# A two-layer decoder trunk on one Trainium2 core: a partial product copied from PSUM bank to PSUM bank in the FFN's Strassen-like blocks, the product order changed, and two waits of the first blocks

## The reference: what is computed

```python
D_MODEL = 1024; SEQ = 512; DEPTH = 2; D_FF = 2816
...
for l in range(DEPTH):
    ...
    x = x + mix @ w_out[l]
    h2 = rms_norm(x, ffn_norm[l])
    gate, up = jnp.split(h2 @ w_gate_up[l], 2, axis=-1)
    x = x + (jax.nn.silu(gate) * up) @ w_down[l]
```

## Time and profile before

| what | value |
|---|---|
| median of 3 runs | 1340.62 us (1340.58 to 1340.69) |
| the profiled execution's own time | 1340.9 us |
| its span in the trace | 1339.2 us |
| PE busy | 1327.0 us, 99% of the span |
| VectorE, ScalarE, GpSimd busy | 791.4, 626.2, 659.8 us |
| chain that ended last | PE 89%, DVE 5%, POOL 2%, ACT 2% |

### The profile page before, as it was taken

The page is one execution under the profiler, slowest core; times in us unless marked ns, Lnnn a source line. Parts: engine busy times, 40 slices in busy tenths (PEclk is TensorE's granted clock), DMA queues, the critical chain, the costliest instruction groups (busy, mean ns, idle before and its releaser), DMA issues.

```text
span 1339.2 us, 22389 instructions
## 1 busy us (share of the span) xinstructions
PE 1327.0 (99%) x8936; PEld 1166.1 (87%) x8936; DVE 791.4 (59%) x1480; ACT 626.2 (47%) x1207; POOL 659.8 (49%) x454
## 2 busy tenths in 40 slices
PE   8999999999999999999999999999999999999999
PEld 7888887778799889998879888887888998899987
DVE  5637777723987138881165387777249861488711
ACT  5563436634556225652335543466335652256511
POOL 4458307644455544554343663176434554454552
PEclk9999999999999999999999999999999999999999
DMA  7315400114243324333222352001232323334322
GB/s 171 124 40 158 102 10 1 33 53 84 76 112 109 104 87 113 109 95 118 87 85 77 75 167 66 1 5 30 63 95 83 107 96 110 95 95 118 104 87 86
DMA packets 176584, 114.92 MB, mean 86 GB/s; under 512 B 48224, under 2 KB 154976, under 8 KB 176480
## 3 DMA queue, kind: packets, MB, share of 16 engines
q1 hardware_dynamic: 174368, 113.22, 29.8%
q10 hardware_dynamic: 2112, 0.26, 0.1%
HBM read 109.80 MB, written 3.67 MB: 85 GB/s over the span
## 4 chain that ended last, share of the span: by engine, by line
PE 89%; DVE 5%; POOL 2%; ACT 2%; issue 1%; DMA 1%; SPq 0%; DVEq 0%; ACTq 0%
PE ps L795 31%; PE ps L1280 29%; PE ps L1181 7%; PE ps L845 6%; PE ps L1082 2%; PE ps L934 2%; PE ps L1125 2%; PE ps L1108 2%; DVE arena L2441 1%; ACT sT_hi L1403 1%; PE ps L860 1%; PE ps L1134 1%; POOL arena L1900 1%; PE ps L914 1%; PE ps L1043 1%
## 5 line engine op out<-in xcount | busy, mean ns | idle before, releaser
L1805 POOL TENSOR_TENSOR w_lo<-w_raw,w_hi 128x2048 fp32r<-128x2048 f32 (+2 forms) x59 | 264.3, 4479 | 313.3 <-ACT w_hi L1382 246.0
L1382 ACT ACTIVATE w_hi<-w_raw 128x2048 fp32r<-128x2048 f32 (+2 forms) x61 | 113.8, 1866 | 236.7 <-PE ps L795 160.8
L1821 POOL TENSOR_TENSOR aT_lo<-ffn_tmp,aT_hi 128x512 fp32r<-128x512 f32 x44 | 58.2, 1322 | 180.7 <-ACT aT_hi L1425 180.7
L2556 DVE SCALAR_TENSOR_TENSOR x_tok<-ps,st,x_tok 128x512 f32<-128x512 f32 x32 | 23.8, 749 | 144.3 <-PE ps L795 144.3
L2459 DVE TENSOR_TENSOR ps<-w_raw 128x512 f32<-128x512 f32 x76 | 88.0, 1158 | 24.3 <-DMA w_raw<-in_w_gate_up 24.3
L795 PE MATMUL ps<-w_hi,aT_hi 128*128 128x512 f32 x352 | 95.8, 390 | 0.0
L795 PE MATMUL ps<-w_lo,aT_hi 128*128 128x512 f32 x352 | 95.4, 389 | 0.0
L795 PE MATMUL ps<-w_hi,aT_lo 128*128 128x512 f32 x352 | 95.4, 389 | 0.0
L795 PE MATMUL ps<-hT_hi,w_lo 128*128 128x512 f32 x320 | 81.0, 393 | 0.0
L1390 ACT ACTIVATE w_hi<-w_raw 128x512 fp32r<-128x512 f32 x38 | 24.0, 632 | 118.4 <-PE ps L1280 89.9
L795 PEld LDWEIGHTS ps<-w_lo,aT_hi 128*128 128x128 f32 x352 | 66.1, 188 | 13.9
(11 more groups left out here) (385 smaller groups left out, 3344.5 us busy)
## 6 DMA issues: line engine op xcount, KB each, us to landing
w_raw<-in_w_gate_up SPq DMA_DIRECT2D x88, 512.0 KB, 5.1
w_raw<-in_w_in SPq DMA_DIRECT2D x21, 1024.0 KB, 5.4
w_raw<-in_w_down SPq DMA_DIRECT2D x16, 1024.0 KB, 5.1
w_raw<-in_w_down SPq DMA_DIRECT2D x8, 768.0 KB, 4.5
w_raw<-in_w_out SPq DMA_DIRECT2D x16, 256.0 KB, 4.0
w_raw<-in_w_out SPq DMA_DIRECT2D x8, 512.0 KB, 5.0
w_raw<-in_w_in SPq DMA_DIRECT2D x2, 1056.0 KB, 7.4
x_tok<-in_x SPq DMA_DIRECT2D x4, 512.0 KB, 5.4
```

Of the source, the lines that this page charges most:

```text
L1382: nc.scalar.activation(whi[:, c % 2, 0:kt * w], raw[:, c % 2, 0:kt * w], ACT.Copy).then_inc(S["w_hi"], 1)
L1805: nc.gpsimd.tensor_tensor(wlo[:, c % 2, 0:kt * w], raw[:, c % 2, 0:kt * w], whi[:, c % 2, 0:kt * w].bitcast(F32), ALU.subtract).then_inc(S ...
L1821: nc.gpsimd.tensor_tensor(alo[:, cnt % FT, :], ft[:, cnt % 2, :], ahi[:, cnt % FT, :].bitcast(F32), ALU.subtract).then_inc(S["a_lo"], 1)
```

## The change

In a fast block, ScalarE copies product one from bank X directly into bank Y (PSUM to PSUM) instead of to SBUF, and TensorE accumulates S2*T2 on top of it. u2_add on VectorE is gone, and with it the SBUF tile p1c. S1*T1 (bank Z) becomes the second product and S2*T2 (bank Y) the third. copy_p5 comes ahead of copy_u2 in ScalarE's list; z_add and t_lo(c + 1, 1) change places in VectorE's. Beside this, plain block 2 no longer waits for gsc and up_mul (i >= 2 becomes i >= 3), since banks 0 and 1 have no earlier block in them; and for block 3 GpSimd does the first quarter's low part ahead of block 1's activation low part.

```diff
 block_product(c, "A11", "B11", X, True, False).then_inc(S["prod"], 1)
 if cnt == N_PLAIN:
-    pe.wait_ge(*S.at("up_mul", N_PLAIN - 1, l))
     pe.wait_ge(*S.at("sum_lo", 4, l))
-elif cnt == FT:
+if cnt == FT:
     pe.wait_ge(*S.at("x_down", 8, l))
-pe.wait_ge(*S.at("sum_lo", 4 + 4 * j + 2, l))
-block_product(c, "S2", "T2", Y, True, False).then_inc(S["prod"], 1)
-if cnt != FT:
+else:
     pe.wait_ge(*S.at("up_mul", halves_done(cnt - 1, 0), l))
+pe.wait_ge(*S.at("sum_lo", 4 + 4 * j + 1, l))
 block_product(c, "S1", "T1", Z, True, False).then_inc(S["prod"], 1)
 pe.wait_ge(*S.at("p_copy", 3 * j + 1, l))
+pe.wait_ge(*S.at("sum_lo", 4 + 4 * j + 2, l))
+block_product(c, "S2", "T2", Y, False, False).then_inc(S["prod"], 1)
 pe.wait_ge(*S.at("w_lo", splits(c), l))
 block_product(c, "A12", "B21", X, False, True).then_inc(S["prod"], 1)
-pe.wait_ge(*S.at("p_copy", 3 * j + 2, l))
+pe.wait_ge(*S.at("p_copy", 3 * j + 3, l))
...
-                        if i >= 2:
+                        if i >= 3:
                             pe.wait_ge(*S.at("up_mul" if s else "gsc", cnt - 1, l))
...
 def copy_p1(cnt):
     act.wait_ge(*S.at("prod", 5 * (cnt - N_PLAIN) + 1, l))
-    nc.scalar.activation(p1c, fast_bank(cnt, "X"), ACT.Copy).then_inc(S["p_copy"], 1)
+    if cnt == N_PLAIN:
+        act.wait_ge(*S.at("up_mul", N_PLAIN - 1, l))
+    elif cnt == FT:
+        act.wait_ge(*S.at("x_down", 8, l))
+    nc.scalar.activation(fast_bank(cnt, "Y"), fast_bank(cnt, "X"), ACT.Copy).then_inc(S["p_copy"], 1)
 def copy_u2(cnt):
-    act.wait_ge(*S.at("p_add", 3 * (cnt - N_PLAIN) + 1, l))
+    act.wait_ge(*S.at("prod", 5 * (cnt - N_PLAIN) + 3, l))
...
 def copy_p5(cnt):
-    act.wait_ge(*S.at("prod", 5 * (cnt - N_PLAIN) + 3, l))
+    act.wait_ge(*S.at("prod", 5 * (cnt - N_PLAIN) + 2, l))
...
+                        copy_p5(cnt)
                         copy_u2(cnt)
...
-                    if fast:
-                        copy_p5(cnt)
...
-                early = cnt is not None and 2 <= cnt < N_PLAIN
-                if early:
+                early = cnt is not None and 2 <= cnt <= N_PLAIN
+                fast = cnt is not None and is_fast(cnt)
+                if early and fast:
+                    block_lo(c, 0)
+                elif early:
                     split_lo(c)
                 if behind is not None:
                     block_a_lo(behind)
-                if cnt is not None and is_fast(cnt):
-                    block_lo(c)
+                if fast:
+                    for part in range(1 if early else 0, 2):
+                        block_lo(c, part)
...
-def u2_add(cnt):
-    dve.wait_ge(*S.at("prod", 5 * (cnt - N_PLAIN) + 2, l))
-    dve.wait_ge(*S.at("p_copy", 3 * (cnt - N_PLAIN) + 1, l))
-    Y = fast_bank(cnt, "Y")
-    V.tensor_tensor(Y, Y, p1c, ALU.add).then_inc(S["p_add"], 1)
...
-                    if fast:
-                        u2_add(cnt)
                     if prepare:
                         t_sum(c + 1, 3)
                         t_lo(c + 1, 0)
+                        t_lo(c + 1, 1)
                     if fast:
                         z_add(cnt)
-                    if prepare:
-                        t_lo(c + 1, 1)
```

More of the change, by code:

```diff
@@ L72 @@
     "x_res": 8, "zgate": 1, "zth": 1,
-    "prod": 95, "p_copy": 57, "p_add": 57, "sum": 77, "sum_hi": 80, "sum_lo": 80,
+    "prod": 95, "p_copy": 57, "p_add": 38, "sum": 77, "sum_hi": 80, "sum_lo": 80,
 }
@@ L262, in trunk @@
         p5c = pbuf[:, 2048:2304]
-        p1c, u2c = (raw[:, s, KD * 256:KD * 256 + 256] for s in range(2))
+        u2c = raw[:, 1, KD * 256:KD * 256 + 256]
         gtm = at(0, NT, 3 * GW)
@@ L1296, in fast_block @@
                 if cnt == N_PLAIN:
-                    pe.wait_ge(*S.at("up_mul", N_PLAIN - 1, l))
                     pe.wait_ge(*S.at("sum_lo", 4, l))
-                elif cnt == FT:
+                if cnt == FT:
                     pe.wait_ge(*S.at("x_down", 8, l))
-                pe.wait_ge(*S.at("sum_lo", 4 + 4 * j + 2, l))
-                block_product(c, "S2", "T2", Y, True, False).then_inc(S["prod"], 1)
-                if cnt != FT:
+                else:
                     pe.wait_ge(*S.at("up_mul", halves_done(cnt - 1, 0), l))
+                pe.wait_ge(*S.at("sum_lo", 4 + 4 * j + 1, l))
                 block_product(c, "S1", "T1", Z, True, False).then_inc(S["prod"], 1)
                 pe.wait_ge(*S.at("p_copy", 3 * j + 1, l))
+                pe.wait_ge(*S.at("sum_lo", 4 + 4 * j + 2, l))
+                block_product(c, "S2", "T2", Y, False, False).then_inc(S["prod"], 1)
                 pe.wait_ge(*S.at("w_lo", splits(c), l))
                 block_product(c, "A12", "B21", X, False, True).then_inc(S["prod"], 1)
-                pe.wait_ge(*S.at("p_copy", 3 * j + 2, l))
+                pe.wait_ge(*S.at("p_copy", 3 * j + 3, l))
                 pe.wait_ge(*S.at("sum_lo", 4 + 4 * j + 4, l))
                 block_product(c, "S3", "T3", Y, False, False).then_inc(S["prod"], 1)
-                pe.wait_ge(*S.at("p_add", 3 * j + 2, l))
+                pe.wait_ge(*S.at("p_add", 2 * j + 1, l))
                 block_product(c, "S4", "B22", Z, False, True).then_inc(S["mm"], 1)
-                pe.wait_ge(*S.at("p_add", 3 * j + 3, l))
+                pe.wait_ge(*S.at("p_add", 2 * j + 2, l))
                 block_product(c, "A22", "T4", Y, False, True).then_inc(S["mm"], 1)
@@ L1806, in split_lo, with block_lo @@
                                         whi[:, c % 2, 0:kt * w].bitcast(F32), ALU.subtract).then_inc(S["w_lo"], 1)
-            def block_lo(c):
+            def block_lo(c, part):
                 dst, src, hi = (slot(v, c, KD, 256) for v in (wlo, raw, whi))
-                pool.wait_ge(*S.at("w_hi", splits(c) - 1, l))
-                nc.gpsimd.tensor_tensor(dst[:, 0:4, 0:P], src[:, 0:4, 0:P], hi[:, 0:4, 0:P].bitcast(F32), ALU.subtract
-                                        ).then_inc(S["w_lo"], 1)
+                if part == 0:
+                    pool.wait_ge(*S.at("w_hi", splits(c) - 1, l))
+                    nc.gpsimd.tensor_tensor(dst[:, 0:4, 0:P], src[:, 0:4, 0:P], hi[:, 0:4, 0:P].bitcast(F32), ALU.subtract
+                                            ).then_inc(S["w_lo"], 1)
+                    return
                 pool.wait_ge(*S.at("w_hi", splits(c), l))
@@ L2499, in gate_up @@
                 if is_fast(cnt):
-                    dve.wait_ge(*(S.at("p_add", 3 * (cnt - N_PLAIN) + 3, l) if h else S.at("mm", mm_count(chunk_of(cnt)) - 1, l)))
+                    dve.wait_ge(*(S.at("p_add", 2 * (cnt - N_PLAIN) + 2, l) if h else S.at("mm", mm_count(chunk_of(cnt)) - 1, l)))
                     g, up = token_half(g, h), p5c if h else fast_bank(cnt, "Z")
```

## The result

The changed kernel takes 1349.12 us in the median (1348.61 to 1351.23, 4 runs), the kernel before, run beside it, 1340.61 us (1340.58 to 1340.69): ratio 1.0066, 95% interval 1.0054 to 1.0079. It is slower by 8.5 us; the forecast was 2.4. The profiled execution took 1349.19 us.

What follows compares the result with a forecast made beforehand. TensorE was taken as the bound, busy 1327.0 of 1339.2 us. Steady blocks 0 and +1.22 a layer, +2.4 in all, gave a 1341.6 span, 1343.3 profiled, 1343.1 for the runs; range 1341.9 to 1346.1.

Steps and rivals of the forecast that it cites:

- Steady blocks cost 0: Fast blocks: new product order and PSUM copy add no TensorE wait, cost 0, the copy's slack being 0.86 us.
- Block 3 starts 2.06 earlier: Without plain block 2's two waits, block 3 starts at 360.23 instead of 362.29, 2.06 us won for the moment.
- The gap moves to S1*T1: Block 3's second product waits for bank Z, released by VectorE's gate_up of block 2; a gap of about 3.5 us.
- the +1.44 a layer: If VectorE's list kept its times, six products instead of five follow the wait in block 3: block 4 starts 1.44 later.
- T3's t_sum of block 3 is stalled by GpSimd: VectorE at 359.05 finds GpSimd in B11's low part, ends at 360.17 instead of 359.74, and is 0.43 late.
- The tie at T1 of block 4 goes to VectorE: VectorE at 363.07 beats GpSimd at 363.08; S1*T1 starts at 365.13, block 4 at 373.85: +1.22 us a layer.
- the other side of the tie: GpSimd gets in first at T1 of block 4: S1*T1 at 366.30, +2.4 a layer; one or both layers, chance 0.27.
- The clock stays full in the new gap: TensorE's clock was taken to stay full behind block 3's gap, adding nothing to the forecast sum.
- rival 4: TensorE's clock falls in block 3's new gap: two slower products a layer, +8.2, 1348.8; one a layer 1346.0; chance 0.05.
- Rivals priced one by one: GpSimd winning the tie (1344.3 or 1345.4, chance 0.27) and the clock falling (1348.8 or 1346.0, 0.05) were priced separately.
- The sum has no term outside the FFN: The forecast added only +1.22 us a layer at block 3 of the FFN, with no term for the mixer.

Runs made afterwards that it cites:

- the filler: Changed kernel plus 16 unused 256-column matmuls in block 3's gap, between the copy of product one and the wait for gate_up: 1347.38 us, ratio 1.0051.

## Why the prediction was wrong, step by step

- **Steady blocks cost 0: right.** 924 matmuls take 110.73 us, the copy from bank to bank 0.37 us, its slack 0.87. Copy and product order are worth nothing to them, for or against: 110.73 us with them and 110.71 without, and with block 3 in TensorE's order 1337.3 and 1337.49 us for the whole kernel.
- **Block 3 starts 2.06 earlier, at 360.23: right.** It starts at 360.17.
- **The gap moves to S1*T1, behind gate_up of block 2: right.** Another bank for it takes 8.6 us off the total. With block 2's waits and GpSimd's old order back, the product order and its copy cost the +1.44 a layer that was worked out.
- **T3's t_sum of block 3 is stalled by GpSimd: right**, 1.12 us, with 1.1 predicted.
- **The tie at T1 of block 4 goes to VectorE: wrong.** This is the step that the forecast rested on. VectorE was 0.02 us behind GpSimd and not 0.01 ahead, and the stall is 1.12 us. S1*T1 starts at 366.25, where the other side of the tie gave 366.30. The size was right and the side was not; hundredths cannot be had from sums of rows that are rounded to hundredths, and the chance of 0.27 for it was too small against 0.50. Two of the kernels above, with the same list up to this point, have VectorE 0.01 to 0.02 us ahead instead. That is +1.1 a layer.
- **The clock stays full in the new gap: wrong.** This is rival 4, to which I gave 0.05. The reason given, that no row of before shows a fall, was no evidence: before had no gap above 0.90 us there. Worth +1.49 and +1.31; the price of one product at the lower level, 1.44 a layer, was the right size. By the Trainium skill (TensorE: Matmul & The Clock Gate, section "What's actually happening") an idle TensorE falls back to the lower clock; the trace agrees, 0.50 behind the gap of 4.49 us.
- **Rivals priced one by one: wrong.** The lost tie and the clock come together, since the tie makes the gap longer. 2 x (1.22 + 1.12) + 1.49 + 1.31 = 7.5: 1348.4 us with the 1.7 around the span and the 1339.2 under it, 0.8 below the profiled 1349.19. No rival had this case, and the range ended at 1346.1. Rival 4 names 1348.8, near the measured 1349.12, but by luck: it has the tie won and two products a layer at the lower level, 2.88 us, where the fall cost 1.3 to 1.5 and the lost tie made up the difference.
- **The sum has no term outside the FFN: wrong by 0.7.** TensorE waits 0.65 us at line 934 in layer 1, in the mixer. It is 0.3 in the kernel with gate_up first, 1.52 in the one with the filler, and absent in all others, also in the one with GpSimd's old order alone, which comes to this place as late as the changed kernel. So the lag is not the cause. The trace names no releaser, but the kernel makes this product wait for eight DMAs out of diag_out, and their times fit. The last is issued near 801.7, the longest takes 4.0 us to land, and the product starts at 805.75. Before, it is issued near 798.4, the longest takes 2.7, and the product starts at 801.18 without a wait. With gate_up first the longest takes 3.5; with the filler it is 3.1, and the DMA that fills diag_out takes 4.4 instead of 2.6. Why one execution has a slower DMA here stays open.

What is shown by undoing one thing: the bank wait, the clock's 1.45 (filler), the place of gate_up behind the contested t_sum (1.65). That the stall's 1.12 is a contest of the two engines is inferred from the pairs of times, and no run undoes it alone: in five kernels, in both layers, whoever has the earlier stamp, by 0.01 to 0.03 us, runs at its own length, and the other pays. The Trainium skill (SBUF — State Buffer, section "Who interferes with whom") says that a VectorE instruction with two SBUF inputs contends with a GpSimd instruction that reads SBUF, and that issue order decides who blocks; all ten pairs agree.

## What to carry to other kernels

Where TensorE is full, a change of order pays only at the edges of the dense stretch. Before such a change, list for every product which instruction of which other engine releases its operand and its bank, and put those instructions in each list in the order in which TensorE asks for them; a single edit moves the wait to the next product that was not moved with it, as it did here three times. A gap on TensorE of 1.9 us or more should be priced with a fall of the clock on top (1.88 us is the shortest behind which a trace here shows one). Gaps are not cheaper for being split: 1.44 and 0.25 us were harmless where 1.85 often was not, but 1.88 and 1.22 us with one product between them cost more than a single gap of 4.49. Where two engines meet within some hundredths of a microsecond, take both outcomes as equally likely, with their consequences.

## What the runs showed of the hardware that was not expected

- The granted clock fell from 1.00 to 0.50 at very different points: 0.7 us after TensorE took up work again in layer 0 of the changed kernel, 0.5 us before it took up work, still in the gap, in layer 1; with gate_up first, 0.4 us after it in layer 0 and 1.3 in layer 1. It came back 3.4 us after each fall, and 6.8 us after it behind the pair of gaps. Gaps and what followed, in the profiled executions: 0.90, 0.48 and 1.42 us in turn, no fall; 1.85, none; 1.88, a fall in one layer and none in the other; 2.43 with filler behind it, none; 2.84 and 4.49, a fall in both layers (though the mean clocks of 0.998 and 0.999 say that most other runs with the 2.84 had less); 1.88 and 1.22 with one product between them, the longest fall, from about 364 to 371.
- A fall costs about the same, 1.3 to 1.5 us, behind 1.88, 2.84 and 4.49 us of gap, and 2.1 to 2.2 behind the pair of gaps.
- With a gap of 1.85 us one and the same kernel has runs with a mean clock of 1.0 and of 0.999, about 1.4 us apart.
- The contest of VectorE and GpSimd is settled by 0.01 to 0.03 us in the records: 0.68 us against 1.80 to 1.82 for the same t_sum, 1.26 to 1.29 against 1.79 to 1.82 for GpSimd's instruction.
- A ScalarE copy of 256 columns takes 0.37 us from PSUM to PSUM, and 0.38 from PSUM to SBUF.
